# Two pairs of products taken out ahead of the first transposes, and steps reordered on three engines in two places

## What is computed

```python
def first_block(x, ...):
    h = rms_norm(x, pre_norm_gain)            # 512 x 1024
    proj = h @ w_in                           # 1024 x 4096: q, k, v, z_a, b, c, u, z_c
    ...                                       # differential attention, gated convolution
    x = x + rms_norm(mixed @ w_out, post_norm_gain)
    e = rms_norm(p @ w_ple_proj, ple_norm_gain)
    return x + sigmoid(x @ w_ple_gate) * e

def second_block(h, ...):
    y = gmlp_mixer(rms_norm_2(h, a_pre_g), a_w_in, ..., a_w_out)
    h = h + rms_norm_2(y, a_post_g)           # the "a" norm, then h3
    kv_in = rms_norm_2(h, kv_norm_g)
    k, v = kv_in @ w_k, kv_in @ w_v           # 1024 x 256 each
    y = swa_mixer(rms_norm_2(h, b_pre_g), k, v, b_w_in, b_sinks, b_w_out)
    return h + rms_norm_2(y, b_post_g)
```

## Time and profile before

| | us |
|---|---|
| median of 3 runs | 872.52 (872.39 to 872.81) |
| the profiled execution | 872.42 |
| its span in the trace | 870.7 |
| TensorE busy | 861.4 (99%) |
| DVE, POOL, ACT busy | 572.5 (66%), 482.4 (55%), 391.0 (45%) |

### The profile page before, as it was taken

How to read it: one execution, slowest core, us unless ns; L and a number is a source line. 1 busy time by engine, 2 the same in 40 slices (tenths; PEclk the granted TensorE clock), 3 DMA queues, 4 the chain that set the end, 5 groups by cost and what they waited for, 6 DMA issues and landing times.

```text
span 870.7 us, 11938 instructions
## 1 busy us (share of the span) xinstructions
PE 861.4 (99%) x4196; PEld 718.0 (82%) x4196; DVE 572.5 (66%) x924; ACT 391.0 (45%) x836; POOL 482.4 (55%) x540
## 2 busy tenths in 40 slices
PE   8999999999999999999999999999999999999997
PEld 6888888888888788888888888888888988888885
DVE  6125647965997489776765535556997487698624
ACT  4123433423667377556112321113787447667622
POOL 7766555682217722318976038871314997666362
PEclk9999999999999999999999999999999999999999
DMA  7543222353971468994743262535973222112202
GB/s 201 169 121 98 74 74 72 124 137 78 220 239 50 142 144 180 217 224 159 168 123 97 66 201 83 136 96 122 239 171 98 73 97 74 49 49 74 73 1 96
DMA packets 83691, 106.84 MB, mean 123 GB/s; under 512 B 11953, under 2 KB 54449, under 8 KB 83634
## 3 DMA queue, kind: packets, MB, share of 16 engines
q1 hardware_dynamic: 72752, 85.12, 30.4%
q0 software_dynamic: 10880, 20.97, 14.2%
q10 hardware_dynamic: 2, 0.00, 0.0%
HBM read 103.98 MB, written 2.10 MB: 122 GB/s over the span
## 4 chain that ended last, share of the span: by engine, by line
PE 93%; DMA 2%; ACT 2%; DVE 1%; issue 1%; POOL 1%; POOLq 0%; DVEq 0%; ACTq 0%; SPq 0%
PE bank L2222 28%; PE bank L2223 27%; PE bank L2224 27%; PE bank L2466 2%; PE bank L2319 1%; PE bank L2494 1%; DMA gcv<-in_w_v 1%; PE bank L2439 1%; PE bank L2489 1%; DMA raw<-in_a_w_out 1%; PE bank L2488 1%; ACT junk L980 1%; PE bank L2430 1%; PE bank L2429 1%; PE bank L2434 1%
## 5 line engine op out<-in xcount | busy, mean ns | idle before, releaser
L880 POOL TENSOR_TENSOR wlo<-raw,whi 128x512 fp32r<-128x512 f32 x180 | 247.2, 1406 | 6.1 <-PE bank L2319 5.2
L871 POOL TENSOR_SCALAR whi<-raw 128x512 fp32r<-128x512 f32 x170 | 119.4, 743 | 170.8 <-PE bank L2224 161.8
L2222 PE MATMUL bank<-actB_hi,whi 128*128 128x512 f32 (+1 forms) x416 | 159.6, 384 | 0.2 <-DVE wlo L1693 0.2
L2223 PE MATMUL bank<-actB_lo,whi 128*128 128x512 f32 (+1 forms) x416 | 158.6, 381 | 0.0
L2224 PE MATMUL bank<-actB_hi,wlo 128*128 128x512 f32 (+1 forms) x416 | 158.5, 381 | 0.0
L2222 PE MATMUL bank<-whi,actA_hi 128*128 128x512 f32 x350 | 138.2, 395 | 0.8 <-DVE actA_lo L1518 0.7
L2224 PE MATMUL bank<-whi,actA_lo 128*128 128x512 f32 x350 | 136.4, 390 | 0.0
L2223 PE MATMUL bank<-wlo,actA_hi 128*128 128x512 f32 x350 | 136.3, 389 | 0.0
L2224 PEld LDWEIGHTS bank<-actB_hi,wlo 128*128 128x128 f32 x416 | 78.2, 188 | 15.1
L2222 PEld LDWEIGHTS bank<-actB_hi,whi 128*128 128x128 f32 x416 | 78.2, 188 | 15.0 <-issue 0.7
L2223 PEld LDWEIGHTS bank<-actB_lo,whi 128*128 128x128 f32 x416 | 78.3, 188 | 14.2
(11 more groups left out here) (275 smaller groups left out, 1641.9 us busy)
## 6 DMA issues: line engine op xcount, KB each, us to landing
raw<-in_a_w_in SPq DMA_DIRECT2D x44, 512.0 KB, 4.2
raw<-in_w_in SPq DMA_DIRECT2D x32, 512.0 KB, 3.9
raw<-in_b_w_in SPq DMA_DIRECT2D x16, 512.0 KB, 3.3
raw<-in_a_w_out SPq DMA_DIRECT2D x12, 512.0 KB, 3.4
gain<-in_a_w_out POOLq DMA_DIRECT2D x9, 512.0 KB, 9.0
raw<-in_w_ple_gate SPq DMA_DIRECT2D x8, 512.0 KB, 5.0
gain<-in_a_w_in POOLq DMA_DIRECT2D x8, 512.0 KB, 7.5
raw<-in_a_w_in POOLq DMA_DIRECT2D x8, 512.0 KB, 7.2
```

The costliest lines, as they stand in the source:

```text
L871: pool.tensor_scalar(H, src[:, i * HALF:(i + 1) * HALF], 1.0, 1.0, ALU.mult, ALU.mult).then_inc(w_hi, 1)
L880: ins = pool.tensor_tensor(L, src[:, i * HALF:(i + 1) * HALF], H.bitcast(f32), ALU.subtract)
L2222: M(out_, whi_, xhi_, start=start, stop=False)
L2223: M(out_, whi_, xlo_, start=False, stop=False)
```

## The change

Five places are edited.

1. `tensor_order`: the second `warm` block (two products of the identity with ones, in four records of the trace) goes. The first stays.
2. POOL: the root of tile 1 of x moves from behind both lower parts of the first half unit to between them.
3. DVE, start: `normed_x(1)` moves ahead of `rest("x", 0, 1)`.
4. ACT, middle: the upper part of the first half of k5, `hi_k5(0)`, moves from behind `normed_n(0)` to behind `turned_n(1)`.
5. DVE, middle: the lower part of the first half of k5 moves from ahead of `add_kept(6, 1, ...)` to behind `h3_in(2)`; `part_gain(2, 0)` moves ahead of `rest_n(1)`.

```diff
@@ tensor_order
-    o += [("warm", 0)] + [("gn", c) for c in range(2)] + [("warm", 1)]
+    o += [("warm", 0)] + [("gn", c) for c in range(2)]
@@ POOL
-            after[0] = [lambda: root("x", 1, D)]
+            after[-0.25] = [lambda: root("x", 1, D)]
@@ ACT
             normed_n(0)
-            hi_k5(0)
             h3_out(1)
             turned_n(0)
             normed_n(1)
             square_a(2, 0)
             turned_n(1)
+            hi_k5(0)
             hi_k5(1)
@@ DVE, start
             rest("x", 0, 0)
+            normed_x(1)
             rest("x", 0, 1)
-            normed_x(1)
             rest("x", 1, 0)
@@ DVE, middle
             lo_two(UNIT_NO["v5", 0], 1)
-            lo_two(UNIT_NO["k5", 0], 0)
             add_kept(6, 1, p03_kept(1), a_out_(3, 0), (c7_made, 42 + 10))
+            part_gain(2, 0)
             rest_n(1)
-            part_gain(2, 0)
             h3_in(2)
-            lo_two(UNIT_NO["k5", 0], 1)
+            for h in range(2):
+                lo_two(UNIT_NO["k5", 0], h)
```

## The result

| | kernel before | changed kernel |
|---|---|---|
| median, us | 872.59 (7 runs, 872.18 to 873.29) | 875.33 (7 runs, 873.17 to 876.58) |
| profiled execution | 872.42 | 876.34 |
| its span | 870.7 | 874.6 |

The ratio is 1.0029, with a 95% interval of 1.0019 to 1.0039. The change made the kernel slower by 2.7 us in the median. The forecast was 872.0 in a range of 871.3 to 873.3, so it was wrong. The spread also grew, from 1.1 to 3.4 us.

A forecast was written before the change was run, and what follows sets the result against it. TensorE was taken to bound the kernel, edits counting only through its waits or queue. Start +0.49 and middle -1.0 gave -0.51 us, so 871.91 profiled and a median of 872.0, range 871.3 to 873.3.

The forecast's parts named there:

- What bounds the kernel: TensorE, busy 861.4 of 870.7 us; an edit is worth only what it does to its waits or queue.
- Start, the queue: Tile 0 goes earlier, but POOL's second lower part ends later and TensorE's third pair waits: +0.49 us.
- the 0.16 for the first record after a gap: At the start, tile 0's transposes lose their place behind running products, so their first record takes 0.16 us more.
- Start, the clock: At the start, a later clock rise got no term in the forecast, only a rival's chance of 0.18.
- The sum: Start +0.49 and middle -1.0 give -0.51 us: profiled execution 871.91, median 872.0.
- rival (a): At the start the clock rises later: +0.9 us and 872.9, or 875.0 if the low level lasts longer; chance 0.18.
- its long form: Low level through the first full block and tile 2's transposes: about 2.1 us more, 875.0; chance 0.05.
- Middle, first and second stall: TensorE's waits before tile 1's transposes (0.82 us, goes whole) and before the k product (starts 667.1 instead of 668.11).
- Middle, what is late next: The chain to tile 2's transposes moves by more than 1.0 us, as `h3_in(2)` moves about 2, so no new wait.
- the term of -1.0: The middle's whole gain, -1.0 us, with bounds -0.66 and -1.14.
- (b): The start costs nothing, POOL's second lower part being done before TensorE wants it: 871.0 to 871.5; chance 0.10.
- (c): The gain is given back at q5, where TensorE wants POOL's lower part near 697 us: 872.6; chance 0.10.

The follow-up runs named there:

- all but the early root: Changed kernel with POOL's root of tile 1 back behind both lower parts: 873.62 us against 872.83 for the kernel before, ratio 1.0012.
- the filled gap: Changed kernel with two idle products inside the first head, ahead of its wait for the weights' lower part: 873.14 against 872.83 us; again 872.68 against 872.39.
- the kernel with the square moved: Kernel before with both middle edits and ACT's square of the mixer's tile 3 ahead of k5's upper parts: 871.39 us against 872.39, ratio 0.9992.
- the run of the middle alone: Kernel before with only the middle's edits (k5's upper and lower parts, gain of tile 2): 872.12 us against 872.57, ratio 0.9997.

## Why the prediction was wrong, point by point

**What bounds the kernel: right in the path, not in what an edit can do to it.** TensorE sets the time. But the prediction said that an edit is worth only what it does to a wait or to TensorE's own queue, and 2.86 of the 3.9 us came from unchanged steps that last longer. A shift of TensorE went through to the end, but for late weights near 345 to 380 us, which moved it from trace to trace. I had taken nothing there. The changed kernel's three traces have +0.6, +0.6 and +0.9 in that stretch, one other (all but the early root) +0.6, and the remaining eight from -0.3 to +0.1, those with the filled gap among them. The DMA engines are busy for 95% of the stretch before and 99% after, but why the transfers land later was not tried and stays open.

**Start, the queue: right in mechanism and nearly in size.** The transposes of tile 0 start at 6.88 (forecast 6.92), the root of tile 1 at 9.42 (9.56), and the third pair waits for POOL at 11.67 (11.83). The term that was off is the 0.16 for the first record after a gap: the eight transposes took 1.81 from their start to the next pair's, against 1.75 before, so they lost 0.06. The queue alone costs 0.33 by this trace, where +0.49 was forecast. The first execution with a filled gap, which had the early rise, has its first full block 0.31 later; the second 1.06 later, since its level rose later and its start was 0.1 later.

**Start, the clock: the step that failed.** The sum took the lengths of TensorE's steps as they were and put nothing for the level of the clock. It was rival (a), with a chance of 0.18, and 0.05 for its long form. In the profiled execution it came as priced: the low level costs 0.46 at the pair and 0.39 at tile 1's transposes, then 1.24 for six products and 0.77 for eight transposes (forecast 2.1 together). What was wrong is the argument against it, that the products at 8.69 put "nearly as much work ahead of the old time of the rise". It weighed only what stood ahead of the rise and not the gap behind it, and even the missing work alone brought 4 late executions of 22. Half of the executions (15 of 30) lie above 874.5; with only one of the two edits of the start it is 2 of 11 each (four kernels), with neither 1 of 95 and none of the 33 of the three kernels with only the middle changed. Both edits count: one takes work away ahead of the old rise, the other has TensorE stand still right behind it. Which of the two matters more, and what decides the form in one execution, stays open. A single profile or three runs would have shown one form or the other. By the Trainium skill (TensorE: Matmul & The Clock Gate, Part 1), activity releases the throttle; the trace agrees in kind, as with 1.0 us of idle products in the gap the level had risen before the first full block. The Trainium skill (TensorE: Matmul & The Clock Gate, Part 1) also puts the cost of the ramp below 1% of a typical kernel's time. That holds here, 2.86 of 872 us being 0.3%, and yet it is more than all else in this change.

**Middle, first and second stall: right.** 0.85 and 0.18 were won in the changed kernel (the forecast's -1.0 is 0.82 and 0.2); in the kernel with the square moved, 1.16 in all.

**Middle, what is late next: the second step that failed.** I wrote that the chain to tile 2's transposes moves by more than 1.0 because `h3_in(2)` moves by about 2. The residual sum and its squares did come early: in the run of the middle alone the squares were done at 667.23, before at 667.74, though that execution came into the middle 0.8 to 1.0 us later. But I counted POOL's root at its length in the rows and not at what stands ahead of it in POOL's queue. The change puts both lower parts of k5 next to the gain of tile 3: three DVE steps with two SBUF inputs, 2.96 us without a break. The prediction names the rule for this (such a DVE step and a POOL step that reads SBUF block each other) and used it at the start alone, for a subtraction that turned out free of it. Where it mattered, it made 0.30 into 3.0 and gave back 0.69 at tile 2 and 0.16 at tile 3. So the term of -1.0 was 0.0 in the trace of the middle alone (from 650 us to behind the transposes of tile 3), and 0.0 to -0.3 in the changed kernel's three. The Trainium skill (SBUF — State Buffer, section Summary: rules for kernel authors) says that, when VectorE has two SBUF inputs and the GpSimd step reads SBUF, the one that issues second blocks until the first finishes; the trace agrees and adds that POOL did not get in between DVE's steps either: 2.99 for a row of three.

**Rivals (b) and (c).** (b) didn't come: POOL's second lower part was wanted before it was done in every trace with the early root but the second filled one, where the filling lasted until it was done. (c) didn't either: no wait for a POOL lower part shows near 697 us, in the changed kernel or in the one with the whole gain of the middle.

**The sum.** For the profiled execution: start +3.2 instead of +0.49 (0.33 for the queue, 2.86 for the clock), middle 0 instead of -1.0, transfers +0.6 instead of 0, and 0.1 behind the middle, in all +3.9 instead of -0.51. No execution of the changed kernel with the early rise was profiled. The 15 at or below 874.5 lie at 872.2 to 874.3, mostly 0.5 to 1.2 above the kernel before, which is what the queue's 0.33 and a middle worth nothing leave, with up to 0.9 for the transfers. So without the clock the time would still have missed the forecast by about 0.8, through the middle, but would have stayed in the range.

## What to carry to other kernels

Idle products in front of real ones should be judged by the lengths of the steps behind them, not by the place they take in the queue, and over ten or more executions: here the cost came in only half of them. A wait of 0.5 to 0.9 us, added where TensorE had so far left its lower level, went with 2.86 us of longer steps in the profiled execution; filled, the kernel's median was 0.3 us above the kernel before. Where such a wait can't be avoided, try filling it. When two-input steps of VectorE are moved next to each other, look for small GpSimd steps that are asked for in that time: here they ended 0.16 us behind the last of the row, and moving what asks for them (here one square of 0.6 us on ScalarE) can free them without taking any work away.

## What the runs showed of the hardware that was not expected

- With two products taken out at the start and 0.5 to 0.9 us of standing still ahead of about 11.8 us, TensorE stayed at its lower level until about 19 us in all three profiled executions; before, it left that level between 10.4 and 11 us. With only a wait of 0.9 or 1.0 us at that place, two traces show the early rise. By the times, the form changes from one execution of the same program to the next, and the long one costs up to about 2.9 us.
- A GpSimd step on one number per partition took 0.29 or 2.99 us at nearly the same place of the program, by whether VectorE had just begun a row of steps with two SBUF inputs; asked for inside such a row, it took 1.34 and 1.45 and ended about 0.16 behind it as well. VectorE's own steps kept their lengths (2.36 for two).
